# Mixture-of-experts routing: hidden rows by products with diagonals, two tiles by one-hot products

## The reference, cut to what matters

```python
h = rms_norm(x, norm_ffn) * (1 + sc2) + sh2      # 512 x 1024
logits = h @ w_router                            # 512 x 8
top_val, top_idx = top_k(logits, 2)
top_w = softmax(top_val)
for e in range(8):                               # D_FF_EXPERT = 1408
    y_e = (silu(h @ gate[e]) * (h @ up[e])) @ down[e]
    out = out + combine[:, e:e+1] * y_e
```

## Time and profile before

| what | value |
|---|---|
| median of 3 runs | 2964.51 us (2963.88 to 2964.90) |
| the profiled execution | 2963.49 us |
| its span, first to last instruction | 2962.1 us |
| PE busy | 2806.0 us, 95% |
| DVE busy | 1695.2 us, 57% |
| ACT busy | 1234.7 us, 42% |
| POOL busy | 227.4 us, 8% |
| mean granted TensorE clock | 0.979 |

### The profile page before, as it was taken

How to read it: one execution, slowest core, us unless ns; L and a number is a source line. 1 busy time by engine, 2 the same in 40 slices (tenths; PEclk the granted TensorE clock), 3 DMA queues, 4 the chain that set the end, 5 groups by cost and what they waited for, 6 DMA issues and landing times. The chain is left out here.

```text
span 2962.1 us, 35850 instructions
## 1 busy us (share of the span) xinstructions
PE 2806.0 (95%) x14515; PEld 2302.8 (78%) x14515; DVE 1695.2 (57%) x2722; ACT 1234.7 (42%) x2009; POOL 227.4 (8%) x209
## 2 busy tenths in 40 slices
PE   7999999999998989899999998999999999999998
PEld 5777788887877888688877775788788767788886
DVE  6785553537846765443578886433425386744344
ACT  3665322224333344233467775432223346432222
POOL 0000000000005441100000010122100000000000
PEclk8999999999999999899999999999999999999999
DMA  5242353422231110244589994211331214322321
GB/s 232 86 148 94 122 201 130 180 73 86 114 121 53 62 44 29 104 178 158 183 329 357 350 371 151 73 60 43 105 116 47 85 40 164 117 86 78 114 82 68
DMA packets 70939, 387.61 MB, mean 131 GB/s; under 512 B 8106, under 2 KB 9806, under 8 KB 35022
## 3 DMA queue, kind: packets, MB, share of 16 engines
q1 hardware_dynamic: 57360, 349.20, 32.5%
q10 hardware_dynamic: 10382, 26.07, 2.6%
q0 software_dynamic: 3024, 9.98, 0.9%
HBM read 368.43 MB, written 22.03 MB: 132 GB/s over the span
## 5 line engine op out<-in xcount | busy, mean ns | idle before, releaser
L340 DVE TENSOR_TENSOR wlo<-stage,whi 128x1024 fp32r<-128x1024 f32 (+3 forms) x481 | 515.7, 1111 | 335.4 <-ACT whi L352 333.6
L352 ACT ACTIVATE whi<-stage 128x1024 fp32r<-128x1024 f32 (+3 forms) x481 | 437.9, 957 | 220.3 <-PE ps L658 199.5
L658 PE MATMUL ps<-whi,mxhi 128*128 128x512 f32 (+1 forms) x528 | 204.4, 387 | 9.9 <-DVE wlo L340 7.8
L658 PE MATMUL ps<-bxhi,whi 128*128 128x512 f32 x480 | 201.5, 420 | 11.1 <-DVE y0lo L340 4.0
L658 PE MATMUL ps<-whi,mxlo 128*128 128x512 f32 (+1 forms) x528 | 197.7, 374 | 0.0
L658 PE MATMUL ps<-wlo,mxhi 128*128 128x512 f32 (+1 forms) x528 | 197.6, 374 | 0.0
L658 PE MATMUL ps<-bxhi,wlo 128*128 128x512 f32 x480 | 191.0, 398 | 0.0
L658 PE MATMUL ps<-bxlo,whi 128*128 128x512 f32 x480 | 190.0, 396 | 0.0
L340 DVE TENSOR_TENSOR wlo<-more,whi 128x1024 fp32r<-128x1024 f32 (+1 forms) x126 | 142.2, 1170 | 44.7 <-ACT whi L352 44.0
L348 DVE SCALAR_TENSOR_TENSOR part<-stage,small,part 128x256 f32<-128x256 f32 x259 | 151.2, 584 | 9.2
L658 PE MATMUL ps<-gwide 128*128 128x128 f32 x1088 | 134.8, 283 | 14.3 <-POOL gwide L340 11.3
(11 more groups left out here) (603 smaller groups left out, 6226.4 us busy)
## 6 DMA issues: line engine op xcount, KB each, us to landing
stage<-in_gu SPq DMA_DIRECT2D x92, 1024.0 KB, 5.2
stage<-in_ada SPq DMA_DIRECT2D x40, 1024.0 KB, 4.8
more<-in_gu SPq DMA_DIRECT2D x40, 1024.0 KB, 6.9
stage<-in_dn SPq DMA_DIRECT2D x26, 768.0 KB, 4.5
stage<-in_dn SPq DMA_DIRECT2D x19, 1024.0 KB, 6.9
stage<-in_gin SPq DMA_DIRECT2D x16, 1024.0 KB, 4.9
stage<-in_gt SPq DMA_DIRECT2D x16, 1024.0 KB, 5.0
more<-in_dn SPq DMA_DIRECT2D x13, 1024.0 KB
```

The lines of the kernel that those rows point to most:

```text
L340: return e.do.tensor_tensor(out, x, y, op)
L352: return e.do.activation(out, x, f, **kw)
L658: return self.p.do.matmul(out, lhsT, rhs, start=start, stop=stop, skip_group_check=True)
```

## The change

- All scores up to block 5 are put between the last 16 steps of `go` (24 of them where 16 were); the four of block 4 no longer follow.
- POOL makes two sets of eight 128x128 diagonal matrices ahead, of the gain and of the shift (gdn_out_pool).
- Instead of norm, shift and transpose: for each half of the features and each 128 tokens, 4 fp32 products x block by gain diagonal (`scaled`) and, added to them, 4 products of the rms, broadcast, by shift diagonal (`shifted`). ACT then copies 128x512 to `rows4` and multiplies by 1/rms per token on the way.
- 1/rms per token comes straight from the squares (8 matmuls of one column) and two small ACT operations; only the rms (for `shifted`) is made for the broadcast form.
- PE's wait on `fence` goes. PE's order: scores 6, scaled x2, scores 7, total, xs4, scaled x4, shifted x4, scaled x2, ranks, shifted x4.
- DVE: ids and flag come straight after the ranks, ahead of places; picks 0 to 3 follow; the shares go behind the branch, after tile 0 and came 2. The first weight piece is split ahead of tile 0, on DVE and ACT.
- Tiles 0 and 1 come from `rows4` in SBUF by 32 fp32 products each with the one-hot matrices (`collect`), with no came, filler or gather DMA. Only tile 2 is gathered by DMA.
- SP: the second half of `rows4` is stored after the first weight piece is asked for; no wait for a gathered tile. ACT waits for both stores before the experts' loop, as `rows4` now lies where it will write.

```diff
@@ gdn_out_pe
             elif k >= 32:
-                self.pe_scores((k - 32) // 4, k % 4)
-        for c in range(4):
-            self.pe_scores(4, c)
+                for u in range((k - 32) * 3 // 2, (k - 31) * 3 // 2):
+                    self.pe_scores(u // 4, u % 4)
+    def gdn_out_pool(self, L):
...
+        g.wait_ge(self.P(("go", "t", 7)), V(("n4", "gain")), V(("mod", 1, 3)))
+        for at, use, cols in ((82, "gains", self.gain(1, 3)), (84, "shifts", self.mod[1][:, 24:32])):
+            diag = self.at(use, [P, 8, P], at)[:, :, :]
+            tt(g, diag, ident, cols.unsqueeze(2).broadcast_to([P, 8, P]), MUL).then_inc(*self.G.up(use))
@@ moe
-        self.banks(range(4))
+        self.banks((3, 0, 1, 2, 1, 2, 4, 5, 6, 7, 3))
@@ route_pe
-        p.wait_ge(*self.fence)
...
+        def scaled(half, c):
+            held[half, c], vacant = self.take(("hr", half, c))
+            p.wait_ge(*vacant, self.G("gains"))
+            for m in range(4):
+                p.wait_ge(V(("go", "x", 4 * half + m)))
+                self.mm(held[half, c][:, m * P:(m + 1) * P], self.x[:, 4 * half + m, blocks[c]], gains[:, 4 * half + m, :], m == 0, False)
+        def shifted(half, c):
+            p.wait_ge(A("sd"), self.G("shifts"))
+            for m in range(4):
+                z = self.mm(held[half, c][:, m * P:(m + 1) * P], L.rs[:, blocks[c]], shifts[:, 4 * half + m, :], False, True)
+            z.then_inc(*P_.up(("hr", half, c)))
+        for c in range(4):
+            self.pe_scores(6, c)
+        scaled(0, 0)
+        scaled(0, 1)
+        for c in range(4):
+            self.pe_scores(7, c)
...
+        for c, s in enumerate(blocks):
+            p.wait_ge(V(("go", "t", 6)))
+            self.mm(ps[:, c:c + 1], self.sq[:, s], self.c("ones")[:, 0:1], True, False)
+            p.wait_ge(self.last_square[1])
+            z = self.mm(ps[:, c:c + 1], self.last_square[0][:, s], self.c("ones")[:, 0:1], False, True)
         self.pe_total("xs4", self.sq, V(("go", "t", 6)), more=self.last_square)
-        for m in range(5):
-            turn(m)
+        for half, c in ((0, 2), (0, 3), (1, 0), (1, 1)):
+            scaled(half, c)
+        for c in range(4):
+            shifted(0, c)
+        scaled(1, 2)
+        scaled(1, 3)
         ps, vacant = self.take("ranks")
...
-        for m in range(5, 8):
-            turn(m)
-        self.pe_came(L, 0)
+        for c in range(4):
+            shifted(1, c)
@@ pe_came
-        self.pe_busy(ps, (2, 3, 0, 0)[n])
@@ route_act
+        act(a, L.rst, self.bank("total")[:, 0:4], ACT.Ln, bias=self.c("e6"), scale=1.0 / 1024).then_inc(*A.up(free("total")))
+        a.wait_ge(A.now())
+        act(a, L.rst, L.rst, ACT.Exp, scale=-0.5).then_inc(*A.up("rst"))
...
+        act(a, L.rs, L.rs, ACT.Exp, scale=0.5).then_inc(*A.up("sd"))
+        for half in range(2):
+            for c in range(4):
...
+                act(a, L.rows4[:, c, 512 * half:512 * half + 512], self.bank(use)[:, :], ACT.Copy, scale=L.rst[:, c:c + 1]).then_inc(*A.up(("hrow", half, c), free(use)))
@@ experts_pe
+        def collect(t):
+            for half in range(2):
+                ps, vacant = self.take(("x", 0, t, 4 * half))
+                p.wait_ge(*vacant, V(("pick", t)), A(("hrow", half, 3)))
+                for m in range(4):
+                    for c in range(4):
+                        z = self.mm(ps[:, m * P:(m + 1) * P], L.rows4[:, c, (4 * half + m) * P:(4 * half + m + 1) * P], L.pick[t][:, c, :], c == 0, c == 3)
+                z.then_inc(*P_.up(("x", 0, t, 4 * half)))
...
+                if i < 2:
+                    collect(t)
+                    continue
...
-        self.pe_came(L, 1)
         gather(0, slice(0, 1))
@@ experts_act
-        gather(0, slice(0, 1))
         self.act_ahead("gu1_0", 0, False)
-        gather(0, slice(1, 4))
+        gather(0)
+        a.wait_ge(*[self.Dh[c]("hrows") for c in range(2)])
@@ experts_dve
-        self.dve_came(L, 1)
+        self.dve_ahead("gu1_0", 0, False)
         gather(0, slice(0, 1))
         for t in range(2, tiles[0]):
             self.dve_came(L, t)
-        self.dve_ahead("gu1_0", 0, False)
+        self.dve_shares(L)
@@ route_sync
+        store(0)
         s.wait_ge(self.V("ids"))
...
         self.sync_load(self.place["gu1_0", 0] + 1)
-        s.wait_ge(self.Dahead[0]("row"))
+        store(1)
         self.sync_load(self.place["gu1_0", 0] + NST)
```

More of the change, by code:

```diff
@@ L1602, in gdn @@
         self.gdn_out_dve(L)
+        self.gdn_out_pool(L)
         self.fence = [s.now() for s in (self.P, self.A, self.V, self.G)]
@@ L2124, in moe @@
         L.pick = [self.at(f"pick{n}", [P, 4, P], 78 + n)[:, :, :] for n in range(4)]
-        L.rows4, L.total, L.rst = rows, self.spare[:, 72:76], self.spare[:, 76:80]
+        L.rows4, L.rst = self.at("mall", [P, 4, 1024], 86)[:, :, :], self.spare[:, 76:80]
         self.Dh = [self.sem(f"hrows{c}") for c in range(2)]
-        self.Dahead = [self.sem(f"ahead{t}") for t in range(3)]
+        self.Dahead = [self.sem("ahead")]
         self.Dsc = [self.sem(f"scatter{i}") for i in range(8)]
@@ L2164, in route_pe @@
[L2164 to L2171, removed]
-        for m in range(5):
-            turn(m)
+        gains, shifts = self.diag
+        held = {}
+        def scaled(half, c):
[4 more added lines that the diff above has]
+                self.mm(held[half, c][:, m * P:(m + 1) * P], self.x[:, 4 * half + m, blocks[c]], gains[:, 4 * half + m, :], m == 0, False)
@@ new lines, in shifted @@
+        def shifted(half, c):
[9 more added lines that the diff above has]
+            self.pe_scores(7, c)
+        ps, vacant = self.take("total")
+        p.wait_ge(*vacant)
@@ L2274, in route_dve @@
         then(v.do.tensor_reduce(rk, w64, AX, ADD))
+        then(tt(v, w64, inner(rk), outer(self.c("io8")), EQ))
+        then(tt(v, w64, w64, inner(self.c("io8")), MUL))
+        then(v.do.tensor_reduce(s8[:, 3, :], w64, AX, ADD))
+        then(v.do.tensor_copy(L.ids, s8[:, 3, :]), "ids")
+        then(tt(v, w64, outer(rk), inner(self.c("io8")), EQ))
+        then(tt(v, w64, w64, inner(self.c("lim")), MUL))
+        then(v.do.tensor_reduce(key, w64, AX, ADD))
+        then(tt(v, key, run, key, GT))
+        then(v.do.tensor_reduce(m3[:, 0:1], key, AX, MAX))
+        then(v.do.tensor_copy(L.flag, m3[:, 0:1]), "flag")
+        then(tt(v, m3, m2, m1, SUB), "gap")
         then(tt(v, w64, outer(rk), inner(self.c("io8")), EQ))
@@ L2294, in pick, with dve_shares, then @@
                 then(ts(v, near, near, 128.0, None, SUB))
[L2296 to L2309, removed]
-            pick(n)
-        then(v.do.tensor_copy(L.idx, s8[:, 5, :]), "idx")
+        for n in range(4):
+            pick(n)
+    def dve_shares(self, L):
+        v, V, A = self.v, self.V, self.A
+        def then(z, *events):
+            z.then_inc(*V.up(*events))
+            v.wait_ge(V.now())
+        then(v.do.tensor_copy(L.idx, L.s8[:, 5, :]), "idx")
         then(ts(v, L.ent[:, 0:8], L.idx, 127, None, ALU.bitwise_and))
```

59 lines of the change are left out of this document (18 added, 41 removed).

## The result

The changed kernel took 2967.73 us (median of 20 runs) against 2963.69 for the one before, measured beside it. The medians lie 4.0 us apart. The ratio is taken over the fast runs alone (two of the 20 of the kernel before took 8154 and 10644 us) and is 1.0020, 95% interval [1.0013, 1.0027], which is 3.8 to 8.0 us. A second measurement, beside the experiments, gave 2968.49 against 2960.10, 1.0027 [1.0017, 1.0037]. Both intervals exclude a ratio of 1. The first ratio lies at the 0.2% that the forecast had as its bound, the second beyond it. The profiled execution took 2968.93 us, span 2967.6, against 2963.49 and 2962.1.

The account below looks back on a forecast made before the run. PE bounds the kernel behind the stage, so the stage's chain sets the end. Terms +1.7 +1.0 +1.0 -2.5 +0 +0.7 -2.6 +5.2 = +4.5 us on the median 2964.51 gave 2969.0 us, range 2961 to 2975.

Parts of the forecast that it names:

- The case that had been given most chance: The forecast itself, whole time 2965 to 2972 us; chance 0.55.
- the clock's 1.0: Ahead of the ranks: half of the 2.1 us that a fall of PE's clock after 24 narrow records would cost, +1.0.
- the branch's zero: From flag to PE's restart: read and branch stay at 4.1 us, change 0, bounds -0.8 and +1.0.
- part 2: Ranks to branch: fewer small DVE operations between copy and flag, -2.5 us; read and branch 0.
- Part 1: Ahead of the ranks: seven more scores +1.7, PE's way to DVE's copy +1.0, the clock +1.0 us.
- rival 2: Ahead of the ranks and in the collects: weight loads pace 128-column products, 3.8 us more, 2972.8; chance 0.03.
- rival 1: Ahead of the ranks: the clock stays low from total on, 10 us over the sum, 2979; chance 0.20.
- Rival 3: PE restarts when pick 0 is there, -0.8, clock losses -2.65 and -1.0 absent; sum 0, 2964.5; chance 0.15.
- Part 3: Branch to tile 1: tile 0's collect +0.7, its first 12 products -2.6, tile 1's collect +5.2 us.
- moved, at no cost: Gathers, POOL's stores of places, SP's store and weight pieces, DVE's shares and ACT's wait shift without cost, 0.
- Rival 4: Collects cheaper than any row, or the weight stream covering the experts' delayed start: 2959.4 or less; chance 0.07.

Follow-up runs that it names:

- quiet: The changed kernel with SP asking for no weights or store between ids and pick 1; 1.0019 of the kernel before.
- busy: The kernel before with three added 1 MB stores into an unused buffer once flag is there; 1.0010 of the kernel before.
- tile1: The changed kernel with tile 1 gathered by DMA again (came and gather), tile 0 still collected by products; 1.0002 of the kernel before.
- flagfirst: The changed kernel with the six operations of flag put ahead of the four of ids; 1.0035 of the kernel before, from six runs.
- idsahead: The kernel before with only ids and flag moved straight behind the ranks, same operations; 0.9999 of the kernel before.

## Why the prediction was right or wrong

The number was right: 2969.0 forecast, 2967.73 measured, no change on the slow side. Against the kernel before it says +4.5; the medians give +4.0, the two ratios +5.9 and +8.0. The case that had been given most chance (2965 to 2972) came in by its time, though not by its way there. Of the sum's eight terms four were within 0.2 us, two were 0.6 and 1.0 off, the clock's 1.0 was not spent, and the branch's zero was 4.45: it was right in part by luck, because the other errors went the other way.

**The step that failed** is the last of part 2: "Read and branch: 0.", with the upper bound "+1.0 if the branch takes as long as DVE's at most did". It measured +4.45 us. The sentence even named the cause, "since weights and a store now move while it is taken"; what was wrong is the row that the upper end was taken from. DVE's 5.09 us of idle time was ended by PE's product, so its own branch was over at some unseen time before. The row that would have told more is PE's own branch by microsecond: a DMA share of 0.00 and 0.03 around the packet (the rows of the kernel before, above). A branch priced in silence was carried into full traffic as if it had a fixed price, and 8.53 us is outside both bounds. quiet and busy show the cause from both sides: 4.09 us with the traffic taken away, 6.50 with traffic put into the kernel before.

**What covered it**, with its sign. The clock did not fall ahead of the ranks in the changed kernel (+1.0 not spent), the way to the copy was 0.6 us shorter than forecast, the link of tile 0's collect 1.0 (it took 9.2 us for 9.95, since the clock came back sooner), and the rest is 0.1 to 0.2 a term. Together -2.7; with +4.45 that makes the +1.7 by which the stage came out longer than the forecast.

**Part 1.** DVE was early at the ranks and waited for PE, as forecast, though for 6.50 us and not the 1.6 that the sum had; what the norms had cost it was worth nothing there. The prices of the 128-column product (32 records in 3.74 us, 0.117; 64 in 7.30, 0.114) held, and rival 2 falls. The clock stayed at 1.00 through the 24 narrow records in the changed kernel and fell in one of the nine profiles with the same order of work up to there, quiet, where it cost 1.5 us: half a chance was too much, and rival 1's 2979 was far. The same instructions can end either way.

**Part 2.** -2.4 for -2.5, the small operations at 0.22 each. Rival 3, that PE had waited for a pick or for `idx`, falls: in the changed kernel pick 0 was there 5.1 us before PE restarted, and in busy, with the code of before, `idx` was there 2.4 us before.

**Part 3.** The collect of tile 0 took 9.2 us of the 9 to 10.5 forecast; tile 1's 7.3 and +5.0 for +5.2 on the path. tile1 turns that around: without it 4.9 us leave that link. The first twelve products ran at full clock in 2.84 us for 2.7. PE did not wait for tile 2's rows. All "moved, at no cost" held, but for one: the second half's store and the weights passed from behind the branch to ahead of the fetch, and I had looked for what is late behind them on SP's queue and not for what shares the DMA engines. Rival 4 had nothing for it and did not come.

What stays open: what makes flagfirst slower than its stage by some 5 us; that q8's packet is PE's code behind the branch, which is inferred from its number and its place and not read from the packet; how much data passes ahead of it, and why 3 MB of stores cost less than 1 MB of a load (6.50 us, 6.73); and whether the whole stage could win if the first weight piece were asked for ahead of the ranks, which needs the sorted experts and was not tried.

## What to carry to other kernels

A branch on a value read at run time had no fixed price here: it took 4.1 us in silence, 6.5 beside 3 MB of stores, 6.7 beside 1 MB and 8.5 beside 4 MB. Read the DMA share over the branch before pricing it, and try to start no bulk load or store in the few microseconds behind the flag, if nothing waits for that load (in quiet PE did). Moving a flag or a number ahead also moves ahead whatever is triggered by it. Trading DVE and DMA time for PE products pays only where DVE or the DMA is last: here PE's own products, 7.3 us for a tile of 128 rows, took the place of a gather that was hidden.

## What was not expected of the hardware

- The code behind a branch comes by DMA, and later beside other traffic: q8's packet stands 2.4 to 3.1 us ahead of PE's restart in every profile, and 1.4 us (no traffic) to 6.1 us (4 MB) behind a `flag` that PE is free to read.
- A read of one word of `flag` from SBUF into a register takes 0.49 us on PE and 0.54 on DVE in most profiles. Twelve such reads, on PE, DVE, ACT and POOL, took 0.99 to 1.59 us, all at a DMA share of 0.84 or more; others at the same share did not grow (DVE's in the changed kernel, 0.54).
- PE's granted clock fell to its lower level (1.2 GHz) during the idle time at the branch, or right behind it (4.5 to 9.8 us), in eleven profiles; in idsahead it had fallen already, behind 4.1 us of waiting for pick 0. Ahead of the ranks it fell in one of nine profiles with the same order of instructions.
